# mLSTM inputs of a block stack on one Trainium2 core: six channel tiles of 128 in place of eight of 96

## The chip, the cores and the metric

The program runs on one core of a Trainium2 chip, in float32 throughout. The core has five engines that run their own instruction streams and meet only at semaphores: TensorE (matmuls, with a weight load of its own for each), VectorE, ScalarE, GpSimd and SyncE, which here only issues transfers. The metric is the device time of one execution of the whole program in microseconds.

## The reference, cut to what matters

The program is a stack of mixers and mixture-of-experts layers over 1024 tokens of width 1024. The change is in the input stage of the second mixer, an mLSTM with 4 heads of 192 channels (ML_W = 768). What this stage has to give:

```python
h = x @ w_in
xm, z, gates, q_mem = jnp.split(h, [ML_W, 2 * ML_W, 2 * ML_W + 4 * ML_HEADS], axis=-1)
xc = lax.conv_general_dilated(xm, conv_w[:, None, :], window_strides=(1,), padding='SAME', ...)   # 5 taps, by channel
xc = jax.nn.silu(xc + conv_b)
q = jnp.einsum('bshd,hde->bhse', xc_h, w_qkv[0])
k = jnp.einsum('bshd,hde->bhse', xc_h, w_qkv[1]) * (ML_DH ** -0.5)
v = jnp.einsum('bshd,hde->bhse', xm_h, w_qkv[2])
g = (gates.reshape(B, S, 4, ML_HEADS) + gate_b).astype(jnp.float32)
```

From the 16 gate columns it also makes log-sigmoids and their cumulative sums within chunks of 128 tokens. The scan that follows wants q and k by feature (channels on partitions) and k and v by token as well.

## The kernel before

The stage is the function `mlstm_inputs` (its tiles are named mi_...). It stands between two barriers that all engines cross (`Stage.__exit__`, lines 55 to 64). x lies transposed in SBUF as `xT` (128 channels x 8 x 1024 tokens).

*Row tiles.* `tiles` is a list of 16 column ranges of `w_in`: eight of 96 for xm, six of 128 for z, two of 128 for the memory queries. The class `Products` (lines 135 to 165) works them off: SyncE loads a tile's weights into one of three buffers, TensorE issues 8 x 2 matmuls of 512 tokens (L158) into one of two accumulators, ScalarE copies the result out (L164), and for the first eight VectorE then runs the five taps of the convolution (L2039, L2041) and ScalarE the SiLU (L1987). With 96 channels to a tile, a head of 192 is two whole tiles.

*Gates.* Before tile 0, TensorE makes the gate logits token block by token block (L1936): the weights are a 128x128 block of `xT`, the moving operand has 16 columns, 64 matmuls. After tile 0 come three matmuls with triangular matrices for the sums (L1943, L1944).

*Products of the heads.* After tiles 3, 5, 7 and 9 (`fm_of`) TensorE makes q and k by feature for one head: four items of two halves of two matmuls, 96 x 96 weights, 512 tokens (L1953), each half in its own bank of `qp`; ScalarE copies them (L1994), scaling k, and GpSimd's queue stores them (L1920). From tile 10 on, three items after each tile (`tm_of`) make k and v by token for two heads and a chunk: eight matmuls of 192 columns (L1966), copied at L2001 and stored at L1925.

*Order.* Each engine's order is written out by hand, as a loop over n = 0 to 15: tile n, then the extra work listed for n. TensorE waits only on semaphores of loads, of copies that free a bank and of SiLUs (`silu`). Every f32 matmul stands in the profile as two records.

*Elsewhere, used for comparison.* L1441 and L1446 (the router's logits: 32-column weights on four column quarters in turn, then turned back), L1711 and L1732 (experts, four lanes of 32 columns), L4305 and L4317 (pairs on 64 columns, pairs on 64 rows) and L667 (64x64 pairs, two heads, both in one bank of `s`).

Of the kernel before, what the change touches and what calls it, by code (L numbers as in the profile page):

```python
# [12 lines left out]
P = 128  # L13
# [1811 lines left out]
QC = 96  # L1825


def mlstm_inputs(nc, xT, w_in, conv_w, conv_b, w_qkv, gate_b, tri, z_out, mq_out, qT_out, kT_out, kx_out, vx_out, xcT_out, ab):
# [3 lines left out]
    NT = C // QC  # L1832
    HEADS, DH = w_qkv.shape[1], w_qkv.shape[2]
    TAPS = conv_w.shape[1]
    PAD = TAPS // 2
    NC = T // P
    SCALE = float(DH) ** -0.5
    w_v = w_in.rearrange("(k p) f -> p k f", p=P)
    G0 = 2 * C
    M0 = G0 + 4 * HEADS  # L1840
# [3 lines left out]
    plain = [z_out[i * P:(i + 1) * P] for i in range(C // P)] + [mq_out[i * P:(i + 1) * P] for i in range(mq_out.shape[0] // P)]  # L1844
    N = len(tiles)
    with Stage(nc, "mi") as s:
        xm = s.sb("xm", [QC, NT, T + 2 * PAD])
        xc = s.sb("xc", [QC, NT, T])
        cw = s.sb("cw", [QC, TAPS, NT])
        cb = s.sb("cb", [QC, NT])  # L1850
        w = s.sb("w", [QC, 3, HEADS, 2, DH])
        wgate = s.sb("wgate", [P, xT.shape[1], 4 * HEADS])
        po = s.sb("po", [P, 2, T])
        qo = s.sb("qo", [QC, 2, T])
        to = s.sb("to", [P, 2, 2, 2 * DH])
        g = s.sb("g", [P, NC, 4, HEADS])
        gb = s.sb("gb", [P, 4 * HEADS])
# [3 lines left out]
        qp = s.ps("qp", [P, 2, BANK])  # L1861
        vp = s.ps("vp", [P, 2, BANK])
        gp = vp[:, 0, 0:NC * 4 * HEADS].rearrange("p (n f) -> p n f", n=NC)
        bp = vp[:, 1, 0:3 * P].rearrange("p (a b) -> p a b", a=3)
        rows = Products(s, xT, tiles)
        (c_loaded, w_loaded, g_loaded, gates, padded, conv, silu, chain, q_done, q_copied, t_done, t_copied, g_exp, g_ln, sums,
         ab_ready, x_stored, g_ready) = (s.sem(n) for n in (
             "c_loaded", "qkv_loaded", "g_loaded", "gates", "padded", "conv", "silu", "chain", "q_done", "q_copied", "t_done",
# [4 lines left out]
        fm = [(h, which, e) for h in range(HEADS) for which in range(2) for e in range(2)]  # L1873
        tm = [(hh, c) for hh in range(2) for c in range(NC)]
        PER_SLOT = 3

        def fm_of(n):

            h = (n - 3) // 2
# [2919 lines left out]
```

## Time and profile before

| | us |
|---|---|
| median of 3 runs | 5991.8 |
| lowest, highest | 5981.63, 5993.96 |
| span of the profiled execution | 5981.1 |
| busy in it: TensorE matmul | 4989.8 (83%) |
| TensorE weight load (beside the matmuls) | 2640.8 (44%) |
| VectorE, ScalarE, GpSimd | 2362.4 (39%), 1213.8 (20%), 624.3 (10%) |
| mean granted TensorE clock | 0.911 |

The profile is of one execution, taken by the hardware profiler. Times of rows are microseconds from the start of its span. PE is TensorE's matmuls, PEld its weight loads, DVE VectorE, ACT ScalarE, POOL GpSimd, SP SyncE; "q" behind an engine's name is its queue. "<-" gives the releaser of a wait. The span is divided among a dozen stages; the one that changes takes 363 us of it, from 1386.8 to 1750.0. TensorE's clock has two levels, shown as a granted clock of 0.50 (1.2 GHz) and 1.00 (2.4 GHz), and means between them for a stretch that has both.

### The profile page before, as it was taken

The numbers are of one execution on the slowest core, as the hardware profiler recorded it, in microseconds if no ns is written. First come the engines' busy times: TensorE is split into PE (matmuls) and PEld (weight loads), VectorE is DVE, ScalarE is ACT, GpSimd is POOL, SyncE is SP. The second block draws the span as 40 slices with busy tenths as digits, with TensorE's granted clock in tenths as the row PEclk, the third lists the DMA queues.
The fourth block names the chain that finished last, engine by engine and source line by source line (L and its number), as shares of the span: only waits on it lengthen the run. The fifth ranks groups of instructions, "written<-read, shape, count | busy, mean of one in ns | idle before, by whom it ended". The sixth has DMA issues, their size and how long they took to land. (4 is left out here: it accounts for less than half of the span.)

```text
span 5981.1 us, 97527 instructions
## 1 busy us (share of the span) xinstructions
PE 4989.8 (83%) x40401; PEld 2640.8 (44%) x40401; DVE 2362.4 (39%) x3801; ACT 1213.8 (20%) x2192; POOL 624.3 (10%) x477
## 2 busy tenths in 40 slices
PE   7998759977988674898588989999489998976798
PEld 4554312224457431232243369999344443322243
DVE  2345510013116662000552756666652641533341
ACT  1223100003111310000431312222211113421111
POOL 0000100000000040000220000000221332311100
PEclk9999879987999786999799999999799999988899
DMA  4111186562334527674431333222501233668620
GB/s 152 50 54 47 64 325 245 205 219 74 95 103 143 160 75 298 245 247 163 130 102 55 137 105 77 66 63 64 218 28 46 74 91 130 211 235 272 228 89 37
DMA packets 580022, 810.59 MB, mean 136 GB/s; under 512 B 174592, under 2 KB 333824, under 8 KB 579144
## 3 DMA queue, kind: packets, MB, share of 16 engines
q1 hardware_dynamic: 515704, 638.54, 32.4%
q0 software_dynamic: 26240, 95.43, 4.5%
q10 hardware_dynamic: 37712, 71.35, 3.2%
q8 instruction: 277, 4.54, 0.3%
q14 instruction: 89, 0.73, 0.0%
HBM read 1366.67 MB, written 199.82 MB: 262 GB/s over the span
## 5 line engine op out<-in xcount | busy, mean ns | idle before, releaser
L158 PE MATMUL ri_acc<-xT,ri_w 128*128 128x512 f32 (+1 forms) x576 | 254.0, 600 | 11.9 <-DMA ri_w<-in_even_w_in 11.9
L648 PE MATMUL na_acc<-xT,na_w 128*128 128x512 f32 x448 | 217.1, 632 | 14.7 <-ACT na_q L716 7.0
L158 PE MATMUL mi_acc<-xT,mi_w 128*96 128x512 f32 (+1 forms) x512 | 224.5, 598 | 0.0
L4455 PE MATMUL le_gp<-le_g,xT 128*128 128x512 f32 x512 | 220.9, 592 | 0.0
L158 PEld LDWEIGHTS ri_acc<-xT,ri_w 128*128 128x128 f32 (+1 forms) x576 | 108.5, 190 | 156.2 <-issue 144.1
L213 PE MATMUL hi_acc<-hi_T,hi_S 128*128 128x512 f32 x384 | 170.0, 592 | 0.0
L1815 DVE TENSOR_TENSOR moe1e_hy<-moe1e_hy,moe1e_u_ps 128x512 f32<-128x512 f32 x20 | 13.8, 688 | 390.9 <-ACT moe1e_hy L1781 377.8
L1711 PE MATMUL moe1e_u_ps<-moe1w_wu,moe1e_xb 128*32 128x512 f32 x1280 | 145.5, 607 | 23.9 <-DMA moe1w_wu<-in_exp_w_up 14.9
L1815 DVE TENSOR_TENSOR moe0e_hy<-moe0e_hy,moe0e_u_ps 128x512 f32<-128x512 f32 x20 | 13.8, 688 | 383.8 <-ACT moe0e_hy L1781 383.8
L780 DVE SCALAR_TENSOR_TENSOR na_e<-na_s,na_bs 128x256 f32<-128x256 f32 (+1 forms) x96 | 47.1, 491 | 295.2 <-PE na_t L674 256.3
L1711 PE MATMUL moe1e_g_ps<-x_tm,moe1e_xb 128*32 128x512 f32 x640 | 144.9, 606 | 20.6 <-DMA xT<-in_exp_w_gate 19.8
L1711 PE MATMUL moe0e_u_ps<-moe0w_wu,moe0e_xb 128*32 128x512 f32 x1280 | 145.4, 607 | 20.1 <-DMA moe0w_wu<-in_exp_w_up 11.4
L1711 PE MATMUL moe0e_g_ps<-x_tm,moe0e_xb 128*32 128x512 f32 x640 | 145.2, 607 | 16.5 <-DMA xT<-in_exp_w_gate 15.8
L1732 PE MATMUL moe1e_y_ps<-moe1e_wd,moe1e_hT 128*32 128x512 f32 x1280 | 146.8, 601 | 13.4 <-DMA moe1e_wd<-in_exp_w_down 10.0
L1732 PE MATMUL moe0e_y_ps<-moe0e_wd,moe0e_hT 128*32 128x512 f32 x1280 | 146.9, 601 | 7.5 <-DMA moe0e_wd<-in_exp_w_down 4.6
L4455 PEld LDWEIGHTS le_gp<-le_g,xT 128*128 128x128 f32 x512 | 96.9, 190 | 120.1 <-issue 120.1
L158 PEld LDWEIGHTS mi_acc<-xT,mi_w 128*96 128x96 f32 (+1 forms) x512 | 91.0, 178 | 128.0 <-issue 128.0
L1711 PE MATMUL moe0e_g_ps<-xT,moe0e_xb 128*32 128x512 f32 x640 | 145.2, 607 | 0.0
L1711 PE MATMUL moe1e_g_ps<-xT,moe1e_xb 128*32 128x512 f32 x640 | 144.9, 606 | 0.0
L648 PEld LDWEIGHTS na_acc<-xT,na_w 128*128 128x128 f32 x448 | 85.1, 199 | 110.3 <-issue 107.8
L4305 PE MATMUL hc_u<-hc_gt,tr_wg 128*64 128x512 f32 x256 | 78.1, 741 | 58.4 <-DMA hc_gt<-scratch_hy_zrows 58.4
L213 PE MATMUL hi_acc<-xT,hi_w 128*128 128x512 f32 x256 | 114.4, 600 | 9.4 <-DMA hi_w<-in_odd_w_in 9.4
(772 smaller groups left out, 9793.1 us busy)
## 6 DMA issues: line engine op xcount, KB each, us to landing
x_tm<-in_exp_w_gate SPq DMA_DIRECT2D x80, 2048.0 KB
xT<-in_exp_w_gate SPq DMA_DIRECT2D x80, 2048.0 KB
moe0w_wu<-in_exp_w_up SPq DMA_DIRECT2D x80, 2048.0 KB
moe0e_wd<-in_exp_w_down SPq DMA_DIRECT2D x80, 2048.0 KB
moe1w_wu<-in_exp_w_up SPq DMA_DIRECT2D x80, 2048.0 KB
moe1e_wd<-in_exp_w_down SPq DMA_DIRECT2D x80, 2048.0 KB
scratch_rk_f<-ri_out POOLq DMA_DIRECT2D x8, 2048.0 KB, 7.0
sc_rx<-scratch_rk_f SPq DMA_DIRECT2D x32, 512.0 KB, 4.8
```

Of the source, the lines that this page charges most:

```text
L158: mm = pe.matmul(self.acc[i % 2][0:n, h * BANK:(h + 1) * BANK], self.wbuf[i % 3][:, k, 0:n], self.rhs[:, k, h * BANK:(h + 1) * BANK], star ...
L213: mm = pe.matmul(self.acc[0:n, bank, :], a[:, k, 0:n], b[:, k, :], start=(first and k == 0), stop=(last and k == KH - 1), skip_group_check ...
L648: mm = pe.matmul(acc[:, h * BANK:(h + 1) * BANK], wt[:, u, :], xT[:, u, h * BANK:(h + 1) * BANK], start=(u == 0), stop=(u == KD - 1))
L780: link(dve.scalar_tensor_tensor(out=e[:, b, live], in0=sp_[:, b, live], scalar=SCALE, in1=bss[j % 2][:, block, table, skipped * KC:(skippe ...
L1711: mm = pe.matmul(ps[part_of[l], :], xb[:, k, part_of[l]], w[l][:, k, :], start=(k == 0), stop=(k == KD - 1))
L1732: mm = pe.matmul(y_ps[part_of[l], c, q * BANK:(q + 1) * BANK], hT[:, k, part_of[l]], wd[l][:, k, q * BANK:(q + 1) * BANK], start=(k == 0), ...
L1815: dve.tensor_tensor(h, h, u_ps[:], ALU.mult).then_inc(h_made, 1)
L4305: mm = pe.matmul(up[gi * CK:(gi + 1) * CK, i % 2, ri, :], wg[:, 2 * slot + gi, ri, :], gt[:, i % 4, gi, :], start=True, stop=True)
L4455: mm = pe.matmul(gp[:, n % 2, h * BANK:(h + 1) * BANK], xT[:, k, n * P:(n + 1) * P], g[:, k, h * BANK:(h + 1) * BANK], start=(k == 0), sto ...
```

## The change

xm is tiled into six tiles of 128 channels (the list `tiles` gets 14 entries). Two heads are now three tiles: the even head has the whole of the first and the low 64 rows of the middle one, the odd head the high 64 rows of the middle one and the whole of the last. The weights are laid out to match: `wf` holds 128 rows of each head, `wp` the 64 remaining rows of two heads one above the other. `by_feature` makes, for two heads and 512 tokens, the first 128 output channels of each (a full product and a 64-row one each, into two banks) and their last 64 channels into the low and the high half of a third bank. `by_tokens` makes k and v of two heads for one chunk of 128 tokens, in two banks. Products of the two heads are issued alternately. All extra work shares one ring of four banks and four output buffers (`ep`, `eo`), numbered by `ExtraUnits`. The scale of k goes into the weights, by VectorE. The gate logits use 32-column weights (16 of the gates, 16 zeros) and 512 tokens as moving operand, on four column quarters in turn, and eight matmuls with `pick` add the quarters and turn them to tokens after tile 0; the sums follow tile 1. k and v are stored by one transfer for each head and chunk. Feature units stand after tiles 4, 5, 7, 8, token units after tiles 6 and 9 to 13.

```diff
+class ExtraUnits:
+
+
+    def __init__(self, units, size):
+        self.first, self.groups, n, m = {}, {}, 0, 0
+        self.per_use = []
+        for u in units:
+            self.first[u], self.groups[u] = n, m
+            self.per_use += [1, 1, 2] if u[0] == "f" else [1, 1]
+            n, m = n + (3 if u[0] == "f" else 2), m + (2 if u[0] == "f" else 1)
+        self.size = size
+
+    def stored_before(self, use):
+
+        return 16 * sum(self.per_use[use % self.size:use:self.size])
+
+    def stored_in(self, slot):
+        return 16 * sum(self.per_use[slot::self.size])
...
-    NT = C // QC
+    NT = C // P
...
-    tiles = [w_v[:, :, i * QC:(i + 1) * QC] for i in range(NT)]
-    tiles += [w_v[:, :, C + i * P:C + (i + 1) * P] for i in range(C // P)]
+    M0 = G0 + GATES
+    assert REST * 2 == P and HEADS == 4 and NT == 6
+    tiles = [w_v[:, :, i * P:(i + 1) * P] for i in range(2 * NT)]
...
+    RING = 4
+    extras = {4: [("f", 0, 0, 0), ("f", 0, 0, 1)], 5: [("f", 0, 1, 0), ("f", 0, 1, 1)], 7: [("f", 1, 0, 0), ("f", 1, 0, 1)],
+              8: [("f", 1, 1, 0), ("f", 1, 1, 1)]}
+    by_token = [("t", g, c) for g in range(2) for c in range(NC)]
+    for n, first, last in ((6, 0, 3), (9, 3, 6), (10, 6, 9), (11, 9, 12), (12, 12, 14), (13, 14, 16)):
+        extras[n] = by_token[first:last]
+    order = [u for n in range(N) for u in extras.get(n, [])]
+    ring = ExtraUnits(order, RING)
...
+        wf = s.sb("wf", [P, 3, HEADS, DH])
+        wp = s.sb("wp", [P, 3, HEADS // 2, DH])
+        wgate = s.sb("wgate", [P, xT.shape[1], QUARTER])
+        pick = s.sb("pick", [P, GATES])
...
+        eo = s.sb("eo", [P, RING, BANK])
...
+        ep = s.ps("ep", [P, RING, BANK])
+        lp, quarters = ep[:, 0:2, :], po[:, 0, :]
+        gp = ep[:, 2, 0:NC * GATES].rearrange("p (n f) -> p n f", n=NC)
+        bp = ep[:, 3, 0:3 * P].rearrange("p (a b) -> p a b", a=3)
...
-                sp.dma_start(wgate[:], w_v[:, :, G0:M0]).then_inc(g_loaded, 16)
+                sp.dma_start(wgate[:, :, 0:GATES], w_v[:, :, G0:M0]).then_inc(wg_loaded, 16)
...
-                    sp.dma_start(w[:, m], w_qkv[m].rearrange("h (j d) e -> d h j e", d=QC)).then_inc(w_loaded, 16)
+                    of_head = w_qkv[m].rearrange("(g a) d e -> a d g e", a=2)
+                    full = wf[:, m].rearrange("p (g a) e -> p a g e", a=2)
+                    sp.dma_start(full[:, 0], of_head[0][0:P]).then_inc(w_loaded, 16)
+                    sp.dma_start(full[:, 1], of_head[1][REST:DH]).then_inc(w_loaded, 16)
+                    sp.dma_start(wp[0:REST, m], of_head[0][P:DH]).then_inc(w_loaded, 16)
+                    sp.dma_start(wp[REST:P, m], of_head[1][0:REST]).then_inc(w_loaded, 16)
...
+                pool.memset(wgate[:, :, GATES:], 0.0).then_inc(zeros, 1)
...
+                        pool.wait_ge(copied, k + 1)
+                        pool.dma_start(out[at:at + P], eo[:, k % RING, :]).then_inc(stored[k % RING], 16)
+                        pool.wait_ge(copied, k + 2)
+                        pool.dma_start(out[at + DH:at + DH + P], eo[:, (k + 1) % RING, :]).then_inc(stored[(k + 1) % RING], 16)
+                        pool.wait_ge(copied, k + 3)
+                        pool.dma_start(out[at + P:at + DH], eo[0:REST, (k + 2) % RING, :]).then_inc(stored[(k + 2) % RING], 16)
+                        pool.dma_start(out[at + DH + P:at + 2 * DH], eo[REST:P, (k + 2) % RING, :]).then_inc(stored[(k + 2) % RING], 16)
...
+                        for a in range(2):
+                            at = (2 * pair + a) * DH
+                            pool.wait_ge(copied, k + a + 1)
+                            pool.dma_start(kv_out.rearrange("m t c -> t m c")[c * P:(c + 1) * P, :, at:at + DH],
+                                           eo[:, (k + a) % RING, 0:2 * DH].rearrange("p (m e) -> p m e", m=2)).then_inc(stored[(k + a) % RING], 16)
...
-                pe.wait_ge(g_loaded, 48)
                 KD = xT.shape[1]
-                for n in range(NC):
-                    for k in range(KD):
-                        mm = pe.matmul(gp[:, n, :], xT[:, k, n * P:(n + 1) * P], wgate[:, k, :], start=(k == 0), stop=(k == KD - 1))
-                mm.then_inc(gates, 1)
+                low, high = slice(0, REST), slice(REST, P)
...
+                def gate_logits():
+                    pe.wait_ge(wg_loaded, 16)
+                    pe.wait_ge(zeros, 1)
+                    for hf in range(T // BANK):
+                        half = slice(hf * BANK, (hf + 1) * BANK)
+                        for k in range(KD):
+                            part = slice(k % 4 * QUARTER, (k % 4 + 1) * QUARTER)
+                            mm = pe.matmul(lp[part, hf, :], wgate[:, k, :], xT[:, k, half], start=(k < 4), stop=(k >= KD - 4))
+                        mm.then_inc(halves, 1)
+
+                def gate_rows():
+                    pe.wait_ge(pick_made, 3)
+                    for n in range(NC):
+                        pe.wait_ge(halves_kept, n * P // BANK + 1)
+                        mm = pe.matmul(gp[:, n, :], quarters[:, n * P:(n + 1) * P], pick[:], start=True, stop=True)
+                    mm.then_inc(gates, 1)
...
+                def free(use):
+                    if use >= RING:
+                        pe.wait_ge(copied, use - RING + 1)
+
+                def by_feature(u):
+                    _, pair, which, half = u
+                    k = ring.first[u]
+                    a, b, both = (ep[:, (k + j) % RING, :] for j in range(3))
+                    x = xc[:, 3 * pair:3 * pair + 3, half * BANK:(half + 1) * BANK]
+                    even, odd = wf[:, which, 2 * pair, :], wf[:, which, 2 * pair + 1, :]
+                    rest = wp[:, which, pair, :]
+                    pe.wait_ge(silu, 3 * pair + 3)
+                    free(k)
+                    pe.matmul(a, even[:, 0:P], x[:, 0, :], start=True, stop=False)
+                    free(k + 1)
+                    pe.matmul(b, odd[:, 0:P], x[:, 2, :], start=True, stop=False)
+                    pe.matmul(a, rest[low, 0:P], x[low, 1, :], start=False, stop=True)
+                    pe.matmul(b, rest[high, 0:P], x[high, 1, :], start=False, stop=True).then_inc(extra, 1)
+                    free(k + 2)
+                    pe.matmul(both[low], even[:, P:DH], x[:, 0, :], start=True, stop=False)
+                    pe.matmul(both[high], odd[:, P:DH], x[:, 2, :], start=True, stop=False)
+                    pe.matmul(both[low], rest[low, P:DH], x[low, 1, :], start=False, stop=True)
+                    pe.matmul(both[high], rest[high, P:DH], x[high, 1, :], start=False, stop=True).then_inc(extra, 1)
+
+                def by_tokens(u):
+                    _, pair, c = u
+                    k = ring.first[u]
+                    pe.wait_ge(silu, 3 * pair + 3)
+                    tok = slice(c * P, (c + 1) * P)
+                    src = [xc[:, 3 * pair:3 * pair + 3, tok], xm[:, 3 * pair:3 * pair + 3, PAD + c * P:PAD + (c + 1) * P]]
+                    out = [[ep[:, (k + a) % RING, m * DH:(m + 1) * DH] for m in range(2)] for a in range(2)]
+                    for a in range(2):
+                        free(k + a)
+                        for m in range(2):
+                            pe.matmul(out[a][m], src[m][:, 2 * a, :], wf[:, 1 + m, 2 * pair + a, :], start=(m == 0), stop=False,
+                                      skip_group_check=True)
+                    for m in range(2):
+                        for a, r in enumerate((low, high)):
+                            mm = pe.matmul(out[a][m], src[m][r, 1, :], wp[r, 1 + m, pair, :], start=False, stop=True, skip_group_check=True)
+                    mm.then_inc(extra, 1)
+
+                gate_logits()
...
+                        gate_rows()
+                    if n == 1:
+                        gate_sums()
+                    if n == 4:
+                        pe.wait_ge(w_loaded, 16 * 12)
+                        pe.wait_ge(w_scaled, 2)
+                        pe.wait_ge(ab_ready, 1)
+                    for u in extras.get(n, []):
+                        (by_feature if u[0] == "f" else by_tokens)(u)
...
+                def keep_extra(u):
+                    k = ring.first[u]
+                    feature = u[0] == "f"
+                    width = BANK if feature else 2 * DH
+                    for j in range(3 if feature else 2):
+                        if (k + j) >= RING:
+                            act.wait_ge(stored[(k + j) % RING], ring.stored_before(k + j))
+                        act.wait_ge(extra, ring.groups[u] + (2 if j == 2 else 1))
+                        act.activation(eo[:, (k + j) % RING, 0:width], ep[:, (k + j) % RING, 0:width], ACT.Copy).then_inc(copied, 1)
...
+                    if i == 0:
+                        dve.wait_ge(w_loaded, 16 * 12)
+                        for x in (wf, wp):
+                            dve.tensor_scalar(x[:, 1], x[:, 1], SCALE, None, ALU.mult).then_inc(w_scaled, 1)
```

## Rows read from the trace of the kernel before

**Rows 1.** Table of stretches of the stage: busy us (instructions) of each engine, granted clock.

```profile
core 0: us, PE busy (x) PEld busy (x) DVE busy (x) ACT busy (x) POOL busy (x), PEclk, DMA share, GB/s
1391.80:1419.10 27.30, 27.29 (x128) 27.29 (x129) 0.00 (x0) 0.00 (x0) 0.00 (x0) 0.50 0.40 92
1419.10:1436.40 17.30, 17.30 (x39) 6.82 (x40) 1.81 (x9) 2.14 (x4) 0.00 (x0) 0.83 0.00 0
...
1477.20:1628.30 151.10, 151.10 (x353) 59.88 (x352) 29.36 (x25) 32.03 (x45) 8.16 (x16) 1.00 0.31 92
...
1739.20:1750.00 10.80, 0.00 (x0) 0.00 (x0) 0.00 (x0) 0.49 (x1) 1.07 (x2) 0.65 0.16 61
```

**Rows 2.** Timeline of TensorE, stage's beginning: start, us, engine, line, operation [idle before].

```profile
1391.81 27.49 PE L1936 MATMUL mi_vp<-mi_wgate,xT 128*128 128x16 f32 x128 [10.65 <-DMA mi_tr<-in_tri]
1419.14 16.82 PE L158 MATMUL mi_acc<-xT,mi_w 128*96 128x512 f32 x32
1435.79 0.53 PE L1943 MATMUL mi_vp<-mi_lf,mi_tr 128*128 128x32 f32 x4
...
1436.41 41.39 PE L158 MATMUL mi_acc<-xT,mi_w 128*96 128x512 f32 x96
```

**Rows 3.** The gate weights' load on SyncE's queue, and its time to landing (min/median/max).

```profile
L1889 SPq DMA_DIRECT2D mi_wgate<-in_ml_w_in x1: 389/389/389, 1386.8 to 1386.8; - x1
...
DMA to landing us min/median/max: 2.3/2.3/2.3
```

**Rows 4.** Timeline of TensorE: two tiles, one head's products, one tile, three token items.

```profile
1573.78 27.63 PE L158 MATMUL mi_acc<-xT,mi_w 128*128 128x512 f32 x64
1601.24 13.91 PE L1953 MATMUL mi_qp<-mi_xc,mi_w 96*96 96x512 f32 x32
1614.99 13.90 PE L158 MATMUL mi_acc<-xT,mi_w 128*128 128x512 f32 x32
1628.73 1.47 PE L1966 MATMUL mi_vp<-mi_w,mi_xc 96*128 96x192 f32 x8
...
1636.53 8.75 PE L158 MATMUL mi_acc<-xT,mi_w 128*128 128x512 f32 x20
```

**Rows 5.** Timeline of TensorE: router's logits of both layers, and what follows them.

```profile
722.75 6.52 PE L1441 MATMUL moe_lp<-xT,moe_rw 128*32 128x512 f32 x32 [6.40 <-DMA moe_rw<-in_router_w]
...
729.20 1.96 PE L1446 MATMUL moe_rp<-moe_pick,moe_quarters 128*128 128x16 f32 x16
...
2237.41 5.25 PE L1441 MATMUL moe_lp<-xT,moe_rw 128*32 128x512 f32 x32 [5.61 <-DMA moe_rw<-in_router_w]
```

**Rows 6.** Timeline of TensorE: pairs on 64 columns, pairs on 64 rows, their successor.

```profile
5351.21 1.94 PE L4305 MATMUL hc_u<-hc_gt,tr_wg 128*64 128x512 f32 x8
5353.08 1.99 PE L4317 MATMUL hc_c<-hc_y,tr_vg 64*128 64x512 f32 x8
5355.00 1.98 PE L4295 MATMUL hc_r<-xT,tr_wr 128*128 128x512 f32 x4
```

**Rows 7.** Timeline of TensorE: one 64x64 pair of 384 columns and its successor.

```profile
299.77 0.86 PE L667 MATMUL na_s<-na_k,na_q 64*64 64x384 f32 x4
300.57 0.55 PE L674 MATMUL na_t<-ident,na_e 128*128 128x128 f32 x3
```

**Rows 8.** Table of stretches: the 64-row pairs of rows 6.

```profile
5353.08:5355.00 1.92, 1.92 (x11) 0.69 (x9) 1.80 (x3) 0.60 (x1) 0.00 (x0) 1.00 0.85 291
```

**Rows 9.** Groups of instructions: count, busy us, mean ns, idle before; landing of the stores.

```profile
L2001 ACT ACTIVATE mi_to<-mi_vp 128x384 f32<-128x384 f32 x32 | 15.6, 491 | 23.2 <-PE mi_vp L1966 20.7 <-DMA scratch_ml_vx<-mi_to 2.5
L1925 POOL DMA_DIRECT2D scratch_ml_kx<-mi_to x16 | 8.7, 542 | 107.3 <-ACT mi_to L2001 107.3
...
L3901 POOL DMA_DIRECT2D scratch_hy_xv<-hi_to x24 | 23.8, 992 | 208.0 <-ACT hi_to L3833 208.0
...
DMA to landing us min/median/max: 2.1/2.3/4.3
```

**Rows 10.** Timeline of TensorE: expert products on four lanes of 32 columns.

```profile
1204.77 3.64 PE L1732 MATMUL moe0e_y_ps<-moe0e_wd,moe0e_hT 128*32 128x512 f32 x32
```

More of the change, by code:

```diff
@@ L1926, in _ @@
-                for b in range(2):
-                    pool.wait_ge(q_stored[b], 16 * (len(fm) // 2))
-                    pool.wait_ge(t_stored[b], 32 * (len(tm) // 2))
+                pool.memset(wgate[:, :, GATES:], 0.0).then_inc(zeros, 1)
+                for u in order:
+                    k = ring.first[u]
+                    if u[0] == "f":
+                        _, pair, which, half = u
+                        out = (qT_out, kT_out)[which][:, half * BANK:(half + 1) * BANK]
+                        at = pair * 2 * DH
+                        pool.wait_ge(copied, k + 1)
[5 more added lines that the diff above has]
+                        pool.dma_start(out[at + DH + P:at + 2 * DH], eo[REST:P, (k + 2) % RING, :]).then_inc(stored[(k + 2) % RING], 16)
+                    else:
+                        _, pair, c = u
[4 more added lines that the diff above has]
+                                           eo[:, (k + a) % RING, 0:2 * DH].rearrange("p (m e) -> p m e", m=2)).then_inc(stored[(k + a) % RING], 16)
@@ new lines, in gate_rows, with gate_sums @@
+                def gate_rows():
[4 more added lines that the diff above has]
+                    mm.then_inc(gates, 1)
+                def gate_sums():
+                    pe.wait_ge(g_ready, 2)
+                    pe.wait_ge(g_loaded, 32)
+                    for d in range(2):
+                        pe.matmul(bp[:, d, 0:NC * HEADS], tr[:, d, :], lf[:, d].rearrange("p n h -> p (n h)"), start=True, stop=True)
+                    pe.matmul(bp[:, 2, 0:2 * NC * HEADS], tr[:, 2, :], lf[:].rearrange("p d n h -> p (d n h)"), start=True, stop=True).then_inc(sums, 1)
@@ L1940, in _ @@
                     if n == 0:
-                        pe.wait_ge(g_ready, 2)
-                        for d in range(2):
-                            pe.matmul(bp[:, d, 0:NC * HEADS], tr[:, d, :], lf[:, d].rearrange("p n h -> p (n h)"), start=True, stop=True)
-                        pe.matmul(bp[:, 2, 0:2 * NC * HEADS], tr[:, 2, :], lf[:].rearrange("p d n h -> p (d n h)"), start=True, stop=True).then_inc(sums, 1)
-                    if fm_of(n):
-                        pe.wait_ge(w_loaded, 48)
@@ L1947, in _ @@
-                    for i in fm_of(n):
-                        h, which, e = fm[i]
-                        pe.wait_ge(silu, 2 * h + 2)
-                        for half in range(T // BANK):
-                            pe.wait_ge(q_copied, max(2 * i + half - 1, 0))
-                            for j in range(2):
-                                mm = pe.matmul(qp[0:QC, half, :], w[:, which, h, j, e * QC:(e + 1) * QC],
-                                               xc[:, 2 * h + j, half * BANK:(half + 1) * BANK], start=(j == 0), stop=(j == 1))
-                            mm.then_inc(q_done, 1)
@@ L1976, in _ @@
+                for hf in range(T // BANK):
+                    act.wait_ge(halves, hf + 1)
+                    act.activation(quarters[:, hf * BANK:(hf + 1) * BANK], lp[:, hf, :], ACT.Copy).then_inc(halves_kept, 1)
                 act.wait_ge(c_loaded, 32)
```

142 lines of the change are left out of this document (50 added, 92 removed).

## Prediction

> **What bounds the kernel now.** I first read the granted clock and the share of TensorE in the page (83%, one core), and then looked for the stage that the diff touches, because an average over a dozen stages says nothing about this one. The table of stretches [rows 1] covers the stage "mi" from the end of the barrier before it (1386.8 us) to the first instruction of the next (1750.0). In every stretch between 1391.8 and 1739.2 (three of them are shown) TensorE's busy time equals the length to within 0.1 us, while the others are idle for most of it (in 151 us VectorE works 29, ScalarE 32, GpSimd 8). So TensorE's own instruction stream is the stage's length, and a microsecond taken out of that stream is a microsecond off the kernel, as long as no other engine takes its place. The stage ends in a barrier, so nothing after it can hide behind it. Second reading: in the first of these stretches TensorE is busy all the time at a granted clock of 0.50, the lower level (1.2 GHz); this is the 27 us of gate products. Third: the timeline of TensorE [rows 2, 4] gives the price of each kind of block as the distance from its start to the start of the next.
>
> **Part 1, the beginning.** Before, TensorE waits for three loads, and the last to land is the table "tri" (the releaser in [rows 2]); it starts at 1391.8. The changed code waits only for the gate weights, issued first at 1386.83 and landing 2.3 us later [rows 3], at 1389.1, and for a memset on GpSimd that has nothing ahead of it. Start at 1389.2: 2.6 us less. (Bounds: 0 if the memset or the load is late, 2.7.)
>
> **Part 2, gates.** Before: 64 matmuls of 16 columns (128 records, since each f32 matmul leaves two), each with its own 128-column weight load, take 1419.14 - 1391.81 = 27.3 us, and the first tile after them takes 1435.79 - 1419.14 = 16.7 us where a tile at the full clock takes 13.7 [rows 2, 4]. After: 16 matmuls of 512 columns with 32-column weights, four column quarters in turn. The same shape and order stands in the routing stage, also after a pause: 32 records, 6.5 us to the end there (722.75 to 729.2), and 5.2 us in the second layer, followed by eight matmuls of 16 columns, 16 records, in 1.9 us [rows 5]. That is exactly what the change issues. I take 6.5 for the logits, the first tile at 13.7 (the clock has come up by then: in [rows 5] the second half of the logits ran faster than the first), and 1.9 for the eight matmuls that turn the sums back, which come after tile 0. Saved: 27.3 + 16.7 - 6.5 - 13.7 - 1.9 = 21.9 us; with 5.2 for the logits 23.2; with a slow tile 0 all the same 18.9. The three cumulative sums move one tile later and cost the same 0.6 us [rows 2]; their wait (VectorE and ScalarE turning gates into logs) has 13.7 us of tile 1 as cover.
>
> **Part 3, two tiles fewer.** A tile is 16 matmuls of 512 columns, however wide the output: (1601.24 - 1573.78)/2 = 13.73 us [rows 4]. The 96-wide ones cost the same: three of them are the 41.39 us of the last line of [rows 2], 13.8 each. Eight become six: 2 x 13.73 = 27.5 us. No bound from below but a new wait (part 6).
>
> **Part 4, q and k by feature.** Before: four blocks of 32 records at 1614.99 - 1601.24 = 13.75 us [rows 4], 55.0 in all. After: eight units, each with two full matmuls, one pair on 64 rows each (low and high, different banks), one pair on 64 columns each, and one pair of 64x64. A pair issued in turns runs side by side in this trace: in the convolution stage four matmuls on 64 columns take 5353.08 - 5351.21 = 1.87 us and four on 64 rows 5355.00 - 5353.08 = 1.92 us [rows 6], where four full ones would be 4 x 0.857 = 3.43. Two pairs are 1.71, so 0.16 to 0.21 us are left over for each change of shape. For 64x64, two heads of 384 columns take 300.57 - 299.77 = 0.80 us [rows 7], where one head alone is 2 x 384 x 0.857/1024 = 0.64 and the two in sequence 1.28: again a pair at the price of one, plus 0.16. A unit is then five times 0.857 and four changes of shape at 0.19: 4.28 + 0.76 = 5.04 us; eight are 40.3. Saved 14.7 us. Bounds: without any cost of change 20.7; with 0.4 for each 8.
>
> **Part 5, keys and values by token.** Before: 7.80 us for three items (1628.73 to 1636.53) [rows 4], 2.60 each, 41.6 for 16. After: per unit eight records of full matmuls and eight of 64 rows that run in pairs, so 12 of 16 slots of 0.1625, 1.95, and two changes of shape, 0.38: 2.33 us; 16 are 37.3. Saved 4.3 us. Bounds: 10.4 without a cost of change; -2 (a loss) at 0.4 each plus nothing else. The scale on the keys moves from ScalarE's copies to two VectorE instructions after the first convolution, under three tiles of 13.7 us before the first use.
>
> **Part 6, what could come late.** *ScalarE:* two copies of 384 elements at 0.49 us per token unit [rows 9] against 2.33, three of 512 at no more than 0.65 (0.49 scaled by the width) per feature unit against 5.0. *GpSimd's queue:* 64 issues instead of 48. The 128-row ones take 0.54 us; one of 1024 pieces takes 0.99 [rows 9]; the new k/v store has 256 pieces, so some 0.6 us, 1.2 per unit of 2.33. *The ring of four banks and buffers:* a token unit takes two, so a bank comes round two units later. Copy, issue and a landing of 2.3 us [rows 9] end some 4 us after the unit, before the second unit after it ends (4.7); so ScalarE is seldom held, and TensorE, which waits for copies and not for stores, later still. A feature unit takes three; the next one's second bank is the one copied first, some 3 us before it is wanted. *SyncE:* twelve loads of the qkv weights in place of three, before tile load 3, which waits for tile 0 anyway. *VectorE:* six convolutions in place of eight, one under each tile. *End:* the tail from the last matmul to the next stage is 10.8 us [rows 1]; the last copy and stores are alike, and four more semaphores are cleared: +0.5 us (0 to 1.5).
>
> **The sum.** 2.6 + 21.9 + 27.5 + 14.7 + 4.3 - 0.5 = 70.5 us. The profiled execution has a span of 5981.1; the median of the runs is 5991.8, so 10.7 us above it. 5981.1 - 70.5 = 5910.6, and plus 10.7 the forecast is 5921.3, say 5921.
>
> **A rule against it.** The 64x64 pair writes one bank from two row halves, on different partitions. The two heads in [rows 7] do the same (both halves of one bank of the scores) and took the time of one. By the Trainium skill, TensorEngine Tiling (Array Packing), section "Restrictions and Gotchas", different row tiles cannot access the same PSUM bank simultaneously; by it the pair would run one after the other. The trace does not agree with it there.
>
> **Rivals.** *(a) The half-row pairs don't run side by side* (in the new units they share accumulations with full products, which no row of before shows). Then part 4 is 54.9 + 8 x 0.76 = 61 us and part 5 is 41.6 + 6: instead of 19.0 saved, 12 lost, and the time is 5921 + 31 = 5952. For it: nothing but the mixture. Against it: [rows 6, 7]. *(b) One bank, one writer:* only the 64x64 pairs run in sequence: 8 x 0.857 = 6.9 us, 5928. Against it: [rows 7]. *(c) Changes of shape are dearer* in short blocks: 0.4 us each, 64 of them, 13 us: 5934. For it: the rows have blocks of two pairs, here they are of one, and a weight load may stay in view each time. *(d) Slower than before: the clock.* [rows 1] shows TensorE busy 27.3 of 27.3 us and the clock still 0.50, so busy is not enough. If stretches with half the array idle were held at the lower level and the clock stayed there under the tiles between them, each full-clock microsecond would cost two. About 266 us of full-clock work remain from tile 0 on; to pass 5992 + 12 they would have to lose 83, which is a mean clock of 266/349 = 0.76 or less; at 0.50 the time is 5921 + 266 = 6187. Against it: the stretch of 64-row pairs ran at a granted 1.00 [rows 8], and the four-lane expert products, 32 records in 3.64 us, at the pace of the full clock [rows 10]. *(e) The packing gives nothing and the tiles don't shrink* is excluded by the code: the tile list is 14 long.
>
> **Chances.** Forecast (5921, own range 5912 to 5932) 0.82; (a) 0.05; (b) 0.04; (c) 0.06; (d) 0.02; 0.01 for waits I don't see. The unknown costs spread the forecast by 5.5 us (the logits and the first tile: -1.3, +3), 6 us (changes of shape) and 2.6 (start); the runs of before differ by 12 us among themselves (5981.6 to 5994.0). Low end: 5921 - 6 - 1 - 8 = 5906. High end: 5921 + 13 + 4 = 5938, which takes in (b) and (c). A measurement here can tell about 0.2% (12 us) from no change; all cases but (d) and the last are faster by more: faster 0.96, within 0.01, slower 0.03.
>
> **What would show it.** In the changed profile: gate products that start near 2.4 us after the first load and end within 7; tiles 13.7 us apart from the first on; 14 tiles; a feature unit of 16 records in 5.0 us, a token unit of 16 in 2.3; a stage of about 293 us from barrier to barrier (363.2 - 70.5). Feature units of 7.6 us would be (a), 5.9 (b), and idle time of TensorE put down to ScalarE's copies or to stores would be a wait that part 6 missed. A granted clock below 1.00 after tile 0 would be (d).

## The result, and the profile after

The changed kernel took 5928.2 us (median of 4 runs, 5922.3 to 5936.9), the kernel before 5990.7 beside it: a ratio of 0.9898, 95% interval [0.9885, 0.9911], so about 61 us less (53 to 69). Timed a second time, beside other runs of the kernel before, the ratio was 0.9898 [0.9882, 0.9915].

The page of the changed kernel has nearly the same shares as before; TensorE is busy 67 us less:

```profile
span 5923.3 us, 97284 instructions
PE 4923.0 (83%) x40257; PEld 2590.2 (44%) x40257; DVE 2351.4 (40%) x3796; ACT 1204.0 (20%) x2182; POOL 639.5 (11%) x494
```

The table of stretches of the changed stage, which answers to [rows 1]; it begins with the first load at 1387.9 and ends with the next stage at 1681.9:

```profile
core 0: us, PE busy (x) PEld busy (x) DVE busy (x) ACT busy (x) POOL busy (x), PEclk, DMA share, GB/s
1387.90:1391.40 3.50, 0.00 (x0) 0.00 (x0) 0.61 (x5) 0.00 (x0) 0.20 (x1) 0.50 0.69 146
1391.40:1396.60 5.20, 5.16 (x32) 1.15 (x32) 0.00 (x0) 0.60 (x1) 0.00 (x0) 0.68 0.95 245
1396.60:1410.50 13.90, 13.90 (x37) 6.21 (x34) 0.00 (x0) 0.60 (x1) 0.00 (x0) 1.00 0.46 134
1410.50:1467.90 57.40, 57.40 (x152) 26.79 (x151) 27.10 (x37) 11.68 (x12) 0.00 (x0) 1.00 0.13 37
1467.90:1668.80 200.90, 200.90 (x673) 95.92 (x671) 11.78 (x10) 40.01 (x67) 38.76 (x62) 1.00 0.35 114
1668.80:1681.90 13.10, 0.11 (x2) 0.00 (x0) 0.00 (x0) 0.91 (x3) 1.49 (x3) 0.59 0.18 58
```

TensorE is still busy from its first product to its last (272.3 us of 272.3 from tile 0 on), so it still sets the stage, and the clock is at 1.00 from tile 0 on. The stage is 293.9 us long in place of 363.2. Its beginning on TensorE, to be held beside [rows 2], then the changes of shape in one feature unit and where the next unit and the next tile start, and the same of a group of three token units, beside [rows 4]:

```profile
1391.44 5.26 PE L1975 MATMUL mi_ep<-xT,mi_wgate 128*32 128x512 f32 x32 [9.19 <-DMA mi_wgate<-in_ml_w_in]
1396.63 14.00 PE L158 MATMUL mi_acc<-xT,mi_w 128*128 128x512 f32 x32
1410.47 1.85 PE L1982 MATMUL mi_ep<-mi_pick,mi_po 128*128 128x16 f32 x16
1412.18 13.98 PE L158 MATMUL mi_acc<-xT,mi_w 128*128 128x512 f32 x32
...
1467.86 1.02 PE L2005 MATMUL mi_ep<-mi_xc,mi_wf 128*128 128x512 f32 x2
...
1469.67 0.69 PE L2008 MATMUL mi_ep<-mi_xc,mi_wp 64*128 64x512 f32 x1
1469.68 0.69 PE L2009 MATMUL mi_ep<-mi_xc,mi_wp 64*128 64x512 f32 x1
...
1470.73 0.64 PE L2011 MATMUL mi_ep<-mi_xc,mi_wf 128*64 128x512 f32 x1
...
1471.74 0.64 PE L2013 MATMUL mi_ep<-mi_xc,mi_wp 64*64 64x512 f32 x1
...
1472.75 1.13 PE L2005 MATMUL mi_ep<-mi_xc,mi_wf 128*128 128x512 f32 x2
...
1477.73 14.00 PE L158 MATMUL mi_acc<-xT,mi_w 128*128 128x512 f32 x32
...
1515.28 0.49 PE L2026 MATMUL mi_ep<-mi_wf,mi_xc 128*128 128x192 f32 x2
...
1516.67 0.60 PE L2030 MATMUL mi_ep<-mi_wp,mi_xc 64*128 64x192 f32 x4
...
1517.53 0.59 PE L2026 MATMUL mi_ep<-mi_wf,mi_xc 128*128 128x192 f32 x2
...
1522.22 14.00 PE L158 MATMUL mi_acc<-xT,mi_w 128*128 128x512 f32 x32
```

Gates 5.2 us and 1.7 after tile 0, where they were 27.3; tile 0 in 13.8. In the feature unit L2008 (low rows) and L2009 (high rows) start 0.01 us apart: the pair runs side by side and takes 1470.73 - 1469.67 = 1.06 us where two in sequence would take 1.71. The first unit takes 1472.75 - 1467.86 = 4.89 us, the two of the group 1477.73 - 1467.86 = 9.87, three token units 1522.22 - 1515.28 = 6.94.

What did not follow is where the rest of the span went. The stage gave 69.3 us, the two profiles' spans differ by 57.8, the timed medians by 62.5 and, the second time, by 65.3. That is the first thing the experiments ask. The second is what the paired products owe to their order, and the third the tail, from TensorE's last product to the next stage, 13.0 us where the kernel before has 10.8 [rows 1].

### The profile page after: what moved, and what is told of

The parts are those of the page before. It is cut to its first block and busy times, and to the rows that moved or that the text cites. A ratio compares the mean times of both kernels' runs of the same rounds, so it can differ in the third digit from the quotient of the medians.

```text
span 5923.3 us, 97284 instructions
## 1 busy us (share of the span) xinstructions
PE 4923.0 (83%) x40257; PEld 2590.2 (44%) x40257; DVE 2351.4 (40%) x3796; ACT 1204.0 (20%) x2182; POOL 639.5 (11%) x494
## 5 line engine op out<-in xcount | busy, mean ns | idle before, releaser
L648 PE MATMUL na_acc<-xT,na_w 128*128 128x512 f32 x448 | 215.4, 628 | 14.7 <-ACT na_q L716 7.0
L158 PE MATMUL mi_acc<-xT,mi_w 128*128 128x512 f32 x448 | 195.4, 595 | 0.0
L1815 DVE TENSOR_TENSOR moe1e_hy<-moe1e_hy,moe1e_u_ps 128x512 f32<-128x512 f32 x20 | 13.8, 688 | 394.1 <-ACT moe1e_hy L1781 381.0
L1815 DVE TENSOR_TENSOR moe0e_hy<-moe0e_hy,moe0e_u_ps 128x512 f32<-128x512 f32 x20 | 13.8, 688 | 386.2 <-ACT moe0e_hy L1781 386.2
L1711 PE MATMUL moe0e_u_ps<-moe0w_wu,moe0e_xb 128*32 128x512 f32 x1280 | 146.6, 611 | 19.4 <-DMA moe0w_wu<-in_exp_w_up 10.7
L158 PEld LDWEIGHTS mi_acc<-xT,mi_w 128*128 128x128 f32 x448 | 84.1, 190 | 106.6 <-issue 106.6
```

The source lines that it names most:

```text
L158: mm = pe.matmul(self.acc[i % 2][0:n, h * BANK:(h + 1) * BANK], self.wbuf[i % 3][:, k, 0:n], self.rhs[:, k, h * BANK:(h + 1) * BANK], star ...
L648: mm = pe.matmul(acc[:, h * BANK:(h + 1) * BANK], wt[:, u, :], xT[:, u, h * BANK:(h + 1) * BANK], start=(u == 0), stop=(u == KD - 1))
L1711: mm = pe.matmul(ps[part_of[l], :], xb[:, k, part_of[l]], w[l][:, k, :], start=(k == 0), stop=(k == KD - 1))
L1815: dve.tensor_tensor(h, h, u_ps[:], ALU.mult).then_inc(h_made, 1)
```

## The experiments

**The two kernels again.** No edit.

> The kernel before, unchanged, for the spread of the stages that the change does not touch. The changed stage ran 69.3 us shorter in the profile (363.2 to 293.95), but the whole span only 57.8 us shorter. Theory A (spread): each of the other stages moves by up to some 5 us from one execution to the next, in both kernels, so a second profile of the kernel before has other stages that differ from the first profile by as much, and in both directions; the changed stage itself repeats within 1 us (363 us). Theory B (the change makes later stages longer by about 10 us, by its layout or its transfers): the later stages of this profile repeat the first one's within 1 to 2 us each, and those of the changed kernel stand apart from both.

> The changed kernel, unchanged, timed more often. Theory A (only the changed stage is shorter, by 69 us; the rest is spread): the ratio lies near 1 - 69/5990 = 0.9885, and the stages after the changed one are on average as long as before. Theory B (some 10 us given back later, each time): the ratio lies near 1 - 59/5990 = 0.990, and the same later stages are the longer ones again (the second expert stage and the two scans, by 4 to 5 us each in the first profile).

The stage took 363.0 us before and 293.3 after. The kernel before had a span of 5995.4 this time, 14 us more than in its first profile, and those 14 us lie in stages that nobody touched. Some of them, from barrier to barrier, us:

| stage | before, three profiles | after, two profiles |
|---|---|---|
| changed stage | 363.2, 363.0, 363.4 | 293.9, 293.3 |
| first experts, with routing | 604.0, 607.8, 600.6 | 607.8, 607.8 |
| second experts, with routing | 615.1, 622.9, 620.4 | 620.8, 619.4 |
| RWKV inputs | 316.5, 316.4, 317.3 | 320.2, 319.1 |
| double scan | 730.9, 732.3, 732.2 | 735.7, 734.8 |
| convolution's last stage | 367.1, 367.7, 364.1 | 362.1, 365.5 |

(The third profile of before is the layout experiment below.) So theory A holds for the most part: the first profile of before was a short one, and single stages differ by up to 8 us between executions. But the ratio came out at 0.9898 once more, not at 0.9885, which lies at the edge of both intervals. Taking each profile's span less its changed stage, the four with tiles of 96 (these three and the gates alone, below) have 5616 to 5632 us, mean 5622; the eight with tiles of 128 have 5626 to 5634, mean 5630. Some us of theory B are thus likely, 8 by these means, though the four have a standard deviation of 7 and four is few. The timed runs say less than that: the gain by ratio falls short of the stage's gain by 8 us both times for the changed kernel, by 6 for the one with stores by SyncE and by 0 for the one with reversed shapes as well (both below), each to within 8 to 10 us by its interval.

By stage, over the twelve profiles, the means differ by more than 1.5 us in three. The first experts (604.1 against 607.3 with tiles of 128; 604 and 607.8 occur with either) run ahead of the changed stage, so no transfer of that stage can be the cause there. The double scan (731.1 against 734.1) runs anywhere from 728.0 to 736.7 with tiles of 128. Only the RWKV inputs keep apart: 316.4 to 317.3 against 319.1 to 320.2, with the old gates in the new stage (below) the one exception, at 317.4.

**One tensor for k and v.** The kernel before, with only the DRAM layout of the changed one:

```diff
-        kx, vx, h_f, h_b = (dram(f"ml_{n}", SEQ, ML_W) for n in ("kx", "vx", "hf", "hb"))
+        kv, h_f, h_b = dram("ml_kv", 2, SEQ, ML_W), dram("ml_hf", SEQ, ML_W), dram("ml_hb", SEQ, ML_W)
+        kx, vx = kv[0], kv[1]
```

> The kernel before with one change outside the stage: kx and vx are the two halves of one DRAM tensor, as in the changed kernel. The stage of the RWKV inputs took 316.4, 316.5 and 317.3 us in three profiles with two tensors and 319.1 to 320.2 in seven with one, and the double scan 729 to 732 and on average 734. If the layout did that, the first takes 319 us or more here, and the changed stage 363; if not, 317 or less, and the 2.7 us belong to something else of the program.

Span 5979.7 us, changed stage 363.4, RWKV inputs 317.3, double scan 732.3. 317.3 is at the upper end of the old kernels and 2 us short of what the layout theory asked for, and the old gates in the new stage (below), which has the one tensor too, took 317.4, so the layout alone is not the cause; what makes the later stages a little longer stays open.

**The gates alone.** Before's kernel with the gate part of the diff (`gate_logits`, `gate_rows`, `gate_sums`, `pick`, the sums' VectorE work after the first convolution), all else as before.

> The kernel before with the new gate logits alone (32-column weights on four column quarters in turn, turned back after tile 0, sums after tile 1); tiles of 96, products and stores as before. From the rows of the changed kernel: start 3.5, logits 5.2, tile 0 13.8, turning back 1.7 us, in place of 5.0, 27.3 and 16.7: 24.7 us shorter, a stage of 338.5 us and a ratio near 0.996. If the gain of the gates hung on the other edits (a wait for the first tile's weights, a log chain that comes late), the stage would be longer than 340 and TensorE idle in it.

Stage 339.5 us, ratio 0.9957 [0.9941, 0.9974]. Stretches of its beginning:

```profile
1384.40:1388.10 3.70, 0.00 (x0) 0.00 (x0) 0.62 (x5) 0.00 (x0) 0.19 (x1) 0.50 0.62 123
1388.10:1393.60 5.50, 5.47 (x32) 1.21 (x32) 0.00 (x0) 0.60 (x1) 0.00 (x0) 0.64 1.00 205
1393.60:1407.40 13.80, 13.80 (x36) 5.33 (x33) 0.00 (x0) 0.60 (x1) 0.00 (x0) 1.00 0.58 121
```

3.7, 5.5 and 13.8 us, close to the 3.5, 5.2 and 13.8 expected, and TensorE is not idle in them: the gates' gain needs none of the other edits. The 23.7 us here are 1 us short of 24.7: the load's landing and the logits, which differ between profiles (below), are 0.5 of it, and the tail, with five more semaphores to clear, 0.3.

**The old gates in the new stage.** The other corner: `gate_logits` replaced by the 64 matmuls with `xT` as weights, `gate_rows` gone.

> The changed kernel with the gate logits of the kernel before (64 matmuls of 16 columns, each with a weight load of 128 columns; all in front of tile 0). If the gates' 24 us are independent of the tiles and the paired products, the stage is 293.6 + 24 = 317.6 us, the other corner of the square whose corners are 363.1 (before), 339.5 (gates alone) and 293.6 (all); clock 0.50 during the gates and coming up some 6 us into tile 0.

```profile
1392.80 27.46 PE L1972 MATMUL mi_ep<-mi_wgate,xT 128*128 128x16 f32 x128 [11.11 <-DMA mi_tr<-in_tri]
```

Stage 319.0 us. The gates are worth 23.6 us with the old tiles (363.1 to 339.5) and 25.4 with the new ones (319.0 to 293.6), the tiles and paired products 44.1 and 45.9: they add up, within 2 us.

**Not in turns.**

```diff
                     pe.matmul(a, even[:, 0:P], x[:, 0, :], start=True, stop=False)
+                    pe.matmul(a, rest[low, 0:P], x[low, 1, :], start=False, stop=True)
                     free(k + 1)
                     pe.matmul(b, odd[:, 0:P], x[:, 2, :], start=True, stop=False)
-                    pe.matmul(a, rest[low, 0:P], x[low, 1, :], start=False, stop=True)
...
-                    for m in range(2):
-                        for a, r in enumerate((low, high)):
+                    for a, r in enumerate((low, high)):
+                        for m in range(2):
```

(and the 64-column products likewise, each head's full-row and 64-row product next to each other)

> The changed kernel with the products on 64 rows or 64 columns no longer issued in turns: each head's are finished before the other's. Same matmuls, same banks, same stores. Theory (in turns they run side by side, otherwise one after the other): a feature unit goes from 4.98 us to 8 x 0.857 plus eight changes of shape at 0.14, 8.0 us (24 us for eight units), a token unit from 2.31 to between 2.7 and 3.0 (6 to 11 us for 16): a stage of 324 to 329 us in place of 294. Rival (the array finds the free half by itself, whatever the order): the stage stays within 3 us of 294, but for some 4 us of more changes of shape.

Stage 319.2 us, 25.6 more. One feature unit of it, and one token unit:

```profile
1468.69 1.02 PE L2005 MATMUL mi_ep<-mi_xc,mi_wf 128*128 128x512 f32 x2
1469.64 1.12 PE L2006 MATMUL mi_ep<-mi_xc,mi_wp 64*128 64x512 f32 x2
1470.69 1.13 PE L2008 MATMUL mi_ep<-mi_xc,mi_wf 128*128 128x512 f32 x2
...
1475.81 1.07 PE L2014 MATMUL mi_ep<-mi_xc,mi_wp 64*64 64x512 f32 x2
1476.81 1.13 PE L2005 MATMUL mi_ep<-mi_xc,mi_wf 128*128 128x512 f32 x2
...
1485.03 13.14 PE L158 MATMUL mi_acc<-xT,mi_w 128*128 128x512 f32 x30
...
1530.43 0.60 PE L2030 MATMUL mi_ep<-mi_wp,mi_xc 64*128 64x192 f32 x4
1530.86 0.50 PE L2030 MATMUL mi_ep<-mi_wp,mi_xm 64*128 64x192 f32 x4
1531.29 0.59 PE L2026 MATMUL mi_ep<-mi_wf,mi_xc 128*128 128x192 f32 x2
```

In the feature unit every product of half an array pays full price, 1.05 us with its change of shape, and the unit takes 1476.81 - 1468.69 = 8.12 us, near the 8.0 expected. The token unit shows something else: the four 64-row matmuls, now low, low, high, high, still take 1531.29 - 1530.43 = 0.86 us, as in turns (1517.53 - 1516.67 = 0.86). So the rival is right for these: among neighbours of one shape, at least in a block of four, the order does not matter, since the high half starts while the low half's second product still waits: the four xc records, low and high, stand ahead of the four xm records, though the low xm product was issued before the high xc one. What costs is a product of another shape between the two halves. The 25.6 us are the feature units': a group of two takes 1485.03 - 1468.69 = 16.34 us in place of 9.87, 25.9 for four groups. (The beginning of this profile, up to tile 0, was 0.4 us shorter than the mean of the two of the changed kernel.)

**Fewer changes of shape.** Every second unit of a group issues its products in the reverse order (64x64 first, full ones last), so that equal shapes meet:

```diff
+                    if flip:
+                        free(k)
+                        pe.matmul(both[low], rest[low, P:DH], x[low, 1, :], start=True, stop=False)
+                        pe.matmul(both[high], rest[high, P:DH], x[high, 1, :], start=True, stop=False)
+                        pe.matmul(both[low], even[:, P:DH], x[:, 0, :], start=False, stop=True)
+                        pe.matmul(both[high], odd[:, P:DH], x[:, 2, :], start=False, stop=True).then_inc(extra, 1)
...
+                        pe.matmul(a, rest[low, 0:P], x[low, 1, :], start=True, stop=False)
+                        pe.matmul(b, rest[high, 0:P], x[high, 1, :], start=True, stop=False)
+                        pe.matmul(a, even[:, 0:P], x[:, 0, :], start=False, stop=True)
+                        pe.matmul(b, odd[:, 0:P], x[:, 2, :], start=False, stop=True).then_inc(extra, 1)
```

> The changed kernel with every second unit of a group in the reverse order of shapes, so that the last shape of one unit is the first of the next: two changes of shape fewer at each of ten joints (4 between feature units, 6 and more between token units: 20 changes in all, as joints within groups of three give one each side). Same matmuls, banks and stores. Theory (a change of shape costs 0.15 us, the difference between the blocks of the changed kernel and the sum of their pairs, e.g. 1.06 for a 64-row pair whose two halves take 0.857): 24 changes at most, 20 at least are gone, 3.0 to 3.6 us: a stage of 290.5 us in place of 293.6 (two profiles: 293.94, 293.26). Rival (the extra 0.15 is a property of the narrow products and not of the change): 293.6.

The count in that text is muddled. There are ten groups; each loses two changes, but the last, which ends the stage, loses one: 19 in all. Stage 290.1 us, 3.5 less, and 3.6 less from tile 0 on (281.6 for 285.2), 0.19 us a change. One group of two feature units, and one of three token units, now full, half | half, full | full, half, each with the tile that follows:

```profile
1468.03 1.02 PE L2028 MATMUL mi_ep<-mi_xc,mi_wf 128*128 128x512 f32 x2
...
1477.66 1.88 PE L158 MATMUL mi_acc<-xT,mi_w 128*128 128x512 f32 x4
...
1514.76 0.49 PE L2053 MATMUL mi_ep<-mi_wf,mi_xc 128*128 128x192 f32 x2
...
1516.15 0.60 PE L2060 MATMUL mi_ep<-mi_wp,mi_xc 64*128 64x192 f32 x4
...
1517.65 0.59 PE L2053 MATMUL mi_ep<-mi_wf,mi_xc 128*128 128x192 f32 x2
...
1521.30 3.27 PE L158 MATMUL mi_acc<-xT,mi_w 128*128 128x512 f32 x7
```

The token group takes 1521.30 - 1514.76 = 6.54 us in place of 6.94, for two changes fewer: 0.20 each. The feature group takes 9.63 in place of 9.87, and the tile behind it, which now follows a product of its own shape, 13.73 in place of 13.84: 0.35 together, 0.17 each. The cost sits in the change, not in the narrow products.

**The tail: stores on SyncE's queue.** The trace holds, beside the instructions that the page counts, a DRAIN of GpSimd at the end of each stage, for which all engines wait at the barrier. Its time and the transfers that GpSimd issued in the stage (start and duration in us):

```
before        1743.07   3.98  GpSimd DRAIN   48 transfers
after         1673.20   5.29  GpSimd DRAIN   64 transfers
before        2098.57   0.71  GpSimd DRAIN    8 transfers, 96 pieces each
before        3167.36   0.71  GpSimd DRAIN    8 transfers, 1024 pieces each
before        3483.44   1.36  GpSimd DRAIN   16 transfers
before        1262.08   1.70  GpSimd DRAIN   20 transfers
```

It goes by 0.083 us a transfer, not by pieces. Two things limit the rule. A stage with 24 transfers has 1.99 us in seven of the twelve profiles and 1.70 in the other five. And where GpSimd ran 15 to 31 TENSOR_TENSOR instructions and issued no transfer, it drained for 1.9 to 2.8 us, so transfers are not all that a drain can wait for. The edit: the bodies of GpSimd's store loop move into SyncE's loop, after the load of tile j + 3 and the store of tile j; the semaphores of the stores are then no longer those kept for GpSimd's transfers, and with none of these in use the end of the stage also leaves out its `dma_reset` (`Stage.__exit__`):

```diff
-        stored = [s.pool_sem(f"stored{b}") for b in range(RING)]
+        stored = [s.sem(f"stored{b}") for b in range(RING)]
...
+                    for u in extras.get(j, []):
+                        store_extra(u)
```

> The changed kernel with the 64 stores of q, k and v issued by SyncE after each tile's loads, and none by GpSimd. Theory (at the end of a stage GpSimd drains for 0.083 us for each transfer it has issued in it: 3.98 us for 48 before, 5.29 for 64 after, and it is in the way of all engines): the drain shrinks below 0.2 us and the tail from the last matmul to the next stage from 12.9 to about 7.5 us; stage 288.2 us, ratio to the kernel before 0.9889. Rival (the drain waits for the last stores to land, whichever queue they are on): the tail stays above 12 us. Second risk: SyncE's queue holds weight loads behind stores, and TensorE gets idle time put down to mi_w.

> The reversed order of shapes and SyncE's stores together: if the two are independent, 3.1 and 5.4 us off 293.6, a stage of 285.1 us and a ratio near 0.9898 - 0.0014 = 0.9884 to the kernel before.

> The changed kernel with k and v stored by a transfer each: 96 transfers on GpSimd's queue in place of 64, the same bytes and the same pieces of 768 bytes. Theory (drain by the number of transfers): 96 x 0.083 = 7.9 us in place of 5.29, and the stage 2.7 us longer, 296.3, plus up to 1 us for the last issues (four at 0.5 in place of two at 0.7). Rival (drain by pieces or bytes): it stays at 5.3 us, the stage within 1 us of 293.6.

The last of these splits each store of k and v in two. Results: stores by SyncE, stage 286.5 us (288.2 was expected), ratio 0.9882 [0.9866, 0.9899]; with the reversed shapes too, stage 285.6, ratio 0.9870 [0.9854, 0.9887], some 78 us below the kernel before and 17 below the changed kernel by ratio (the first interval still holds the changed kernel's 0.9898, so the gain of SyncE's stores alone is shown by the stage and not by the time); k and v apart, stage 297.9 and 2.5 us longer from tile 0 on than the changed kernel, its drain 7.90 us. The tails, from the last product to the next stage, of the last, the first and the second of these:

```profile
1673.40:1688.80 15.40, 0.00 (x0) 0.00 (x0) 0.00 (x0) 0.88 (x3) 2.75 (x6) 0.60 0.13 45
...
1669.80:1676.00 6.20, 0.00 (x0) 0.00 (x0) 0.00 (x0) 0.89 (x3) 0.00 (x0) 0.73 0.25 83
...
1668.10:1674.10 6.00, 0.00 (x0) 0.00 (x0) 0.00 (x0) 0.77 (x2) 0.00 (x0) 0.79 0.26 88
```

With 96 transfers the drain is 7.90 us, as counted (96 x 0.083); with none on GpSimd's queue there is no drain over 0.3 us left and the tail is 6.2 instead of 13.0. Of these 6.7 us the drain is 5.3; the missing `dma_reset`, which drains once more (0.42 us, L59), is some 0.8, and the last stores are done 0.65 us sooner after the last product. A drain that waits for landings would not go from 5.29 to 7.90 with the same bytes, and in the changed kernel GpSimd's own wait for the last landing ended at 1673.0, before the drain began at 1673.2. SyncE's loads never held TensorE: in the list of waits of that kernel no wait of TensorE is on a transfer of `mi_w`, and only ScalarE waits once, 8.3 us, for a store:

```profile
ACT mi_eo L2060 <- DMA scratch_ml_kv<-mi_eo: 8.3, 1, 8.3
```

With both edits the stage is 285.6 us, near the expected 285.1 but less than 1 us below the stores alone. The reason is the beginning: in this profile the gate weights' load took 4.3 us to TensorE's first product, and the logits 6.4, 10.7 in all; with the stores alone 8.0. From tile 0 to the next stage the two gains add in full: 285.2 us in the changed kernel, 281.6 with the shapes reversed, 278.5 with SyncE's stores, 274.9 with both (3.6 + 6.7 = 10.3 less).

## Why the prediction was right

It said 5921 us (5906 to 5938), a gain of 70.5 us; 5928 was measured, with 61 us by the ratio. The time alone does not decide for the forecast: rival (b) asked for 5928 too. What decides is the stage, 293.9 us where about 293 was said, and its units, 4.9 to 5.0 us where (b) asked for 5.9. Term by term, in the changed stage:

| term | predicted | measured |
|---|---|---|
| start to the first product | -2.6 | -1.5 (4.98 to 3.53) |
| gates and tile 0 | -21.9 | -23.2 |
| two tiles fewer | -27.5 | -27.5 |
| q and k by feature | -14.7 | -15.5 (eight units 39.5) |
| k and v by token | -4.3 | -4.6 (16 units 37.0) |
| tail | +0.5 | +2.1 |
| tiles next to another shape | 0 | +1 (13.84 for 13.73) |
| stage | -70.5 | -69.3 |

That the sum is off by only 1.2 us is luck in part: the start, the tail and the tiles cost 3.7 us more than was said, and the gates and the units gave 2.4 us more.

*Start.* The row of the gate weights' landing was one execution. In eight profiles with the new wait the first product came 2.3 us after the load's issue four times and 3.5 to 4.3 the other four times; with the old wait 5.0 to 5.7. The direction held and the gain is 0.7 to 3.4 us.

*Gates.* The logits took 5.2 us, the second of the two rows in [rows 5] and not the first, which the sum used. When the clock rises within them is the whole difference: over the eight profiles with the new gates they took 5.2 us at a granted clock of 0.68 (here) to 6.4 at 0.55, and clock times length is 3.5 us in each.

*Tiles.* As predicted. *Feature and token units.* The price of a change of shape was taken from three blocks of two other stages, 0.19, and is 0.17 to 0.20, if the 0.1 us is counted that a tile loses behind another shape. The sum put that at the units alone: they and the tiles together gave 19.1 us (15.5 + 4.6 - 1.0), and 19.0 was said. The price is the same in short blocks as in long ones, so rival (c) falls. Rival (a) falls with the pairs that start 0.01 us apart. The condition in it, that they share accumulations with full products, did not matter. Rival (b) falls with the 64x64 pair, 1472.75 - 1471.74 = 1.01 us: two row halves wrote one bank, on different partitions, at the price of one product plus a change of shape. The rule of the Trainium skill that the prediction quoted from TensorEngine Tiling (Array Packing), section "Restrictions and Gotchas" does not hold for such a pair; the measurement decides. The same page says, in "Key Properties", that changing the tiling mode drains TensorE; by this the trace agrees: each change costs 0.17 to 0.20 us here. Rival (d) falls with a granted clock of 1.00 from tile 0 on, over 272 us, in which some 38 us, a seventh, went to products on part of the array (8 x 3.08 in the feature units, 16 x 0.86 in the token units).

*Tail.* The one term that came out beyond its own bounds (0 to 1.5): the prediction counted the semaphores to clear and the last stores, and not GpSimd's drain, which [rows 1] holds only as a stretch in which nothing is busy. 1.3 of its 2.1 us are the drain for 16 more transfers; 0.3 are the four semaphores, 0.1 a longer drain at L59, and 0.4 the last copies and stores, whose issue took 0.71 us each where part 6 had 0.6.

*From the stage to the kernel.* The sum was made against a profile whose span was among the lowest (5981.1, where the second profile had 5995.4) and then moved up to the median, which was right. It took every other stage as unchanged; by the twelve profiles some 8 us came back there, by the ratios 0 to 8. With 8 the forecast would have been 5929. Whether it is a part of the change or the scatter of those stages stays open; only the layout of k and v was tried, and it is not the cause.

## What to carry to other kernels

Where one engine is busy throughout a stage, price the stage block by block from the distance between starts of the same shape elsewhere in the trace, and the sum can come out within 2%, as it did here. Products that use half the array cost half only if their partner is next to them in the same shape; group by shape, and count some 0.19 us for each change. At the end of a stage, look for what the engines wait for while the page shows nothing busy: here each transfer on GpSimd's queue cost 0.083 us there, and moving 64 of them to SyncE's queue, which had room, was worth 6.7 us of the stage.

## What the runs showed of the hardware

- GpSimd's drain at the end of a stage lasted some 0.083 us for each transfer it had issued: 0.71 us for 8, 3.98 for 48, 5.29 for 64, 7.90 for 96, whether a transfer has 96 or 1024 pieces, and the drain of this stage is gone when it issued none. With 24 it was 1.99 or 1.70, and behind TENSOR_TENSOR instructions alone 1.9 to 2.8.
- Four 64-row products in the order low, low, high, high ran as fast as in turns (0.86 us both ways). Two of 64 rows with one full product between them ran one after the other, each at full price.
- A change of shape (full array, 64 rows, 64 columns, 64x64) cost 0.17 us each between feature units and 0.20 between token units, 0.19 on average over the 19 taken away; a part of it, 0.1 us, is paid by the full tile behind a narrower product (13.84 us for 13.73).
- Stages that nobody touched differ by up to 8 us between executions of one kernel (615.1 and 622.9 us for the second experts), so a difference of spans between two profiles says less than the stage's own length, which repeated within 0.7 us, and within 0.1 from tile 0 on in the changed kernel (285.22 and 285.21).
- Two products of 64 rows and 64 columns, one on each half of the rows, wrote one PSUM bank on different partitions at the price of one (1.01 us with a change of shape).
